# Put-off modulation sums, latent norms by halves, and a shorter last norm in a two-block transformer kernel

## Chip, cores and metric

One core of one Trainium2 chip runs the whole program in one launch. The metric is device time in microseconds (us), the median of the runs that were timed. All inputs lie in HBM and are read once; one sequence of 256 positions with 1024 features goes through.

## The reference

The first part has two layers, each with two feed-forward networks ("ffn0" to "ffn3" in the kernel) around a mixer: a windowed mean in layer 0, causal attention with 8 heads in layer 1. The second part is one block with a state-space branch, an attention branch over latents (16 heads), gates and an output projection. Every sublayer starts with an RMS norm whose scale and shift come from the conditioning vector `c`:

```python
c_silu = jax.nn.silu(c)
mods = jnp.split(c_silu @ ada_w[layer] + ada_b[layer], N_MOD, axis=-1)   # 1024 x 9216
h = modulate(rms_norm(x, norm_g[layer, 0]), sh, sc)                      # norm * (1 + sc) + sh
x = x + 0.5 * (1.0 + g)[:, None, :] * swiglu(h, w_in, w_out)
...
h = _rmsnorm(x, g_pre[l]) * (1.0 + scale[:, None]) + shift[:, None]
u_s, z_s, q_lat, kv_lat, k_rope, z_m, gl_s, gl_m = jnp.split(h @ w_in[l], split_at, axis=-1)
q = (_rmsnorm(q_lat, g_q_norm) @ w_q_up).reshape(bsz, seq, MLA_HEADS, QK_NOPE + QK_ROPE)
kv = (_rmsnorm(kv_lat, g_kv_norm) @ w_kv_up).reshape(bsz, seq, MLA_HEADS, QK_NOPE + V_HEAD)
...
out = merged @ w_out[l]
x = x + gate[:, None] * _rmsnorm(out, g_post[l])
```

## The kernel before

**Layout.** Everything is kept transposed: features on the 128 partitions (8 tiles, `KT`), the 256 positions along the row. Weights come as a stream of "units" of 128 x 1024 numbers (512 KB). SyncE loads a unit into one of 4 landing slots (`load_unit`, L349), ScalarE rounds it to its high part (`split_hi`, writes w_hi, L355), VectorE takes the rest (`split_lo`, writes w_lo, L359), and TensorE makes three products for each 128 x 128 block of it (`products`, L367 to L369): high by high, low by high, high by low. One unit is 24 such matmuls of 256 columns. The order on each engine is written out by hand; semaphores join them. Slot and ring have 4 entries, so a load waits for the VectorE split four units earlier, and `split_hi` waits until TensorE has used the unit four earlier.

**Modulation sums.** The conditioning products (`c_silu @ ada_w`) come in 46 blocks of 512 columns (`g_load`, 2 MB each). VectorE multiplies and adds 8 rows of a block (`g_part`, L1361 and L1364, into one of two accumulators, `g_acc`), and TensorE then sums over partitions with 4 matmuls against ones (`reduce_block`, L524, writes mods; each shows as 2 records). In a feed-forward network (`ffn`) this is done beside the 22 hidden tiles: the loops over hidden tiles (`SEGMENTS`) handle 4 tiles a pass, 12 units and 2 blocks, so TensorE meets one block every 6 units.

**Norms.** After a feed-forward network VectorE updates x, ScalarE squares it, TensorE sums the squares over partitions (`sum_squares`, L534), ScalarE takes the root (L1031 or L1338), VectorE the reciprocal (`root`, L1407), and then each tile is scaled (L1417) and split into x_hi (ScalarE, L1045) and x_lo (VectorE, L1424). `gate_coef` and `norm_coef` make the coefficients from mods.

**Latents.** In the second block the unit order is lat (4), kr (1), u (6), qup (4), kvup (4), u2 (2), zm (8). The lat tiles are normalised while TensorE does the u units: squares L1237, sums L893, root L1251, one reciprocal over 512 columns L1736, four scalings L1738, four copies to a_hi L1256, four a_lo L1715. The qup matmuls wait for all four a_lo, the kvup matmuls follow. Into this stretch fall also the sine of the rotary angles (ScalarE, L1241), the skip term of the state-space response (L1730), the storing of that response to HBM (L461) and eight loads that bring it back in shifted copies (`toep`, L469), all on SyncE's one queue.

**End.** The eight tiles of the output projection are copied from PSUM (L1100), squared (L1336), summed (L534), and after root and reciprocal VectorE scales each tile (L1884), adds it to x (L1888), and SyncE stores it (L514).

## Time and profile before

| | before |
|---|---|
| timed runs | median 1452.31 us (1451.8 to 1453.49, 3 runs) |
| the profiled execution | 1457.6 us, span 1455.8 us |
| mean granted TensorE clock | 0.964 of full |
| TensorE matmul busy | 1337.4 us, 92% of the span |
| VectorE / ScalarE / GpSimd busy | 77% / 43% / 11% |
| DMA | 318.06 MB, mean 218 GB/s |
| chain that ended last | PE 76%, DVE 12%, ACT 5%, issue 4% |

PE is TensorE, DVE VectorE, ACT ScalarE, POOL GpSimd and SP SyncE. The chain is the sequence of work followed back from the last instruction, so a share there is time that the end depends on, while a busy share alone is not. The span begins and ends with the program's instructions; the time of an execution has a little more around it.

### The profile page before, as it was taken

How to read it: one execution, taken by the hardware profiler on the slowest of the kernel's cores; microseconds unless marked ns; L12 is line 12 of the kernel's file. 1: busy time of each engine (PE TensorE's matmuls, PEld its weight loads, DVE VectorE, ACT ScalarE, POOL GpSimd, SP SyncE). 2: the span in 40 equal slices, each digit the busy share in tenths (PEclk: the TensorE clock that was granted, in tenths of full speed). 3: DMA queues.
4: the chain of work that ended last, by engine and by line, in shares of the span. 5: the costliest groups of instructions: out<-in, count | busy, mean ns of one | idle time of the engine just before them, and what ended most of it. 6: DMA issues, size and time to landing. Idle time of an engine off the chain costs nothing.

```text
span 1455.8 us, 28146 instructions
## 1 busy us (share of the span) xinstructions
PE 1337.4 (92%) x10988; PEld 1297.0 (89%) x10988; DVE 1118.1 (77%) x1697; ACT 625.0 (43%) x948; POOL 163.0 (11%) x209
## 2 busy tenths in 40 slices
PE   3899999799999897999998889999996898999996
PEld 2799998799999877999998779999996787999996
DVE  6898777797777787877777657899965777886573
ACT  3333334433333534333344553433364456355443
POOL 6891000000000020000001000000001002331000
PEclk9899999799999998999999899999998999999998
DMA  9788787278876455887753237886655278455551
GB/s 368 258 333 298 288 289 273 90 276 313 289 288 232 128 175 200 338 303 289 290 156 114 71 143 279 342 293 232 210 160 150 78 152 145 140 174 182 166 186 47
DMA packets 91286, 318.06 MB, mean 218 GB/s; under 512 B 21920, under 2 KB 34496, under 8 KB 85056
## 3 DMA queue, kind: packets, MB, share of 16 engines
q1 hardware_dynamic: 91200, 316.87, 63.7%
q8 instruction: 59, 0.97, 0.3%
q14 instruction: 27, 0.22, 0.0%
HBM read 311.82 MB, written 5.01 MB: 218 GB/s over the span
## 4 chain that ended last, share of the span: by engine, by line
PE 76%; DVE 12%; ACT 5%; issue 4%; DMA 1%; POOL 1%; SPq 0%; DVEq 0%; ACTq 0%; POOLq 0%
PE tiles L367 16%; PE tiles L369 15%; PE tiles L368 15%; PE acc L367 6%; PE acc L369 6%; PE acc L368 6%; ACT w_hi L355 2%; PE mods L524 2%; DVE arena L1364 2%; DVE w_lo L359 2%; PE nrm L534 1%; PE tiles L557 1%; PE tiles L559 1%; PE acc L677 1%; DMA land<-in_stream 1%
## 5 line engine op out<-in xcount | busy, mean ns | idle before, releaser
L359 DVE TENSOR_TENSOR w_lo<-land,w_hi 128x1024 fp32r<-128x1024 f32 x391 | 483.0, 1239 | 204.7 <-ACT w_hi L355 202.3
L355 ACT CAST w_hi<-land 128x1024 fp32r<-128x1024 f32 x391 | 408.5, 1046 | 525.6 <-PE tiles L369 286.1
L367 PE MATMUL tiles<-x_hi,w_hi 128*128 128x256 f32 x1464 | 419.3, 286 | 7.6 <-ACT arena L1100 3.9
L368 PE MATMUL tiles<-x_lo,w_hi 128*128 128x256 f32 x1464 | 415.0, 283 | 0.0
L369 PE MATMUL tiles<-x_hi,w_lo 128*128 128x256 f32 x1464 | 414.9, 283 | 0.0
L367 PEld LDWEIGHTS tiles<-x_hi,w_hi 128*128 128x128 f32 x1464 | 281.6, 192 | 11.5 <-ACT arena L1100 4.1
L368 PEld LDWEIGHTS tiles<-x_lo,w_hi 128*128 128x128 f32 x1464 | 281.6, 192 | 1.1 <-issue 1.0
L369 PEld LDWEIGHTS tiles<-x_hi,w_lo 128*128 128x128 f32 x1464 | 281.5, 192 | 0.0
L1364 DVE SCALAR_TENSOR_TENSOR arena<-arena,csil 128x512 f32<-128x512 f32 x280 | 212.5, 759 | 2.0
L367 PE MATMUL acc<-h_hi,w_hi 128*128 128x256 f32 x704 | 202.3, 287 | 0.3 <-DVE h_lo L1383 0.3
L367 PE MATMUL tiles<-a_hi,w_hi 128*128 128x256 f32 (+1 forms) x656 | 188.9, 288 | 13.7 <-DVE a_lo L1715 12.4
L369 PE MATMUL acc<-h_hi,w_lo 128*128 128x256 f32 x704 | 199.2, 283 | 0.0
L368 PE MATMUL acc<-h_lo,w_hi 128*128 128x256 f32 x704 | 199.1, 283 | 0.0
L368 PE MATMUL tiles<-a_lo,w_hi 128*128 128x256 f32 (+1 forms) x656 | 186.5, 284 | 0.0
L369 PE MATMUL tiles<-a_hi,w_lo 128*128 128x256 f32 (+1 forms) x656 | 186.5, 284 | 0.0
L367 PEld LDWEIGHTS tiles<-a_hi,w_hi 128*128 128x128 f32 (+1 forms) x656 | 125.7, 192 | 15.9 <-issue 12.8
L367 PEld LDWEIGHTS acc<-h_hi,w_hi 128*128 128x128 f32 x704 | 135.1, 192 | 0.4 <-issue 0.4
L368 PEld LDWEIGHTS acc<-h_lo,w_hi 128*128 128x128 f32 x704 | 135.1, 192 | 0.0
L369 PEld LDWEIGHTS acc<-h_hi,w_lo 128*128 128x128 f32 x704 | 135.0, 192 | 0.0
L368 PEld LDWEIGHTS tiles<-a_lo,w_hi 128*128 128x128 f32 (+1 forms) x656 | 125.8, 192 | 0.7 <-issue 0.7
L369 PEld LDWEIGHTS tiles<-a_hi,w_lo 128*128 128x128 f32 (+1 forms) x656 | 125.8, 192 | 0.0
L1100 ACT ACTIVATE arena<-tiles 128x256 f32<-128x256 f32 (+4 forms) x81 | 35.3, 435 | 102.7 <-PE tiles L369 94.8
(328 smaller groups left out, 1680.5 us busy)
## 6 DMA issues: line engine op xcount, KB each, us to landing
land<-in_stream SPq DMA_DIRECT2D x391, 512.0 KB, 4.3
arena<-in_gstream SPq DMA_DIRECT2D x46, 2048.0 KB, 8.8
w_dram<-arena SPq DMA_DIRECT2D x3, 512.0 KB, 6.3
arena<-w_dram SPq DMA_DIRECT2D x6, 256.0 KB, 11.0
x<-in_x_t SPq DMA_DIRECT2D x1, 1024.0 KB, 14.0
arena<-in_ssm_bn SPq DMA_DIRECT2D x1, 1024.0 KB, 5.6
u_dram<-arena SPq DMA_DIRECT2D x1, 1024.0 KB, 5.3
arena<-u_dram SPq DMA_DIRECT2D x8, 128.0 KB, 6.3
```

The source lines that it names most:

```text
L355: nc.scalar.copy(w_hi[:, u % RING], land[:, u % LAND]).then_inc(hi_done, 1)
L359: nc.vector.tensor_tensor(w_lo[:, u % RING], land[:, u % LAND], w_hi[:, u % RING].bitcast(F32), ALU.subtract).then_inc(lo_done, 1)
L367: nc.tensor.matmul(outs, lh, rh, start=first, stop=False, **kw)
L368: nc.tensor.matmul(outs, lh, rl, start=False, stop=False, **kw)
L369: last = nc.tensor.matmul(outs, ll, rh, start=False, stop=end, **kw)
L524: m = nc.tensor.matmul(mods[:, bass.ds(i * 8 + (4 * b + q), 1)], g_acc[:, b % 2, q * P:(q + 1) * P], ones[:, 0:1], start=True, stop=True)
L534: m = nc.tensor.matmul(nrm[:, 0:T], ones, t_buf[:, k], start=(k == 0), stop=(k == KT - 1))
L557: nc.tensor.matmul(outs[c], lh, hi[:, k], start=(k == 0 and not (c and one_bank)), stop=False, skip_group_check=True)
L559: nc.tensor.matmul(outs[c], ll, hi[:, k], start=False, stop=False, skip_group_check=True)
L677: m = nc.tensor.matmul(acc4[:, h, qt * T:(qt + 1) * T], qq[0:parts, 2 * g + h, qt * P:(qt + 1) * P], kk[0:parts, 2 * g + h, :], start=True ...
L1100: nc.scalar.activation(dst, src, func, **kw).then_inc(freed["a"], 1)
L1364: V.scalar_tensor_tensor(out=acc, in0=rows, scalar=cv, in1=acc, op0=ALU.mult, op1=ALU.add).then_inc(g_done if k == 7 else g_step, 1)
```

## The change

Five things change. (1) The last four blocks of modulation sums of ffn0, ffn1 and ffn2, and the last two of ffn3 (`LATER`), are no longer summed by TensorE inside the loops but after the next `sum_squares` (`reduce_later`); the first twelve of them get four accumulators of their own (`late_acc`), and the loops are cut into 3 + 1 + 1 passes so that the last two can differ. `gate_coef(1, ...)` moves behind the norm since it needs one of these blocks. (2) The latent norm is made by halves and stands ahead of a weight split on VectorE; the qup matmuls wait for the two q latents alone and the kvup matmuls for the other two. (3) On SyncE the qup units are loaded ahead of the store of the response, and its eight reloads come after the first four zm units. (4) The sine is taken ahead of ffn2. (5) The last norm: the square is taken straight from PSUM, the copy applies the gain, VectorE adds seven of the eight squares so that TensorE sums in two matmuls, the root's table is fetched early, and the final scaling and addition go over 4, 2 and 2 tiles at once with three stores.

```diff
-SEGMENTS = [[(5, "silu")], [(5, "silu")], [(5, "silu")], [(1, "silu"), (1, "c2"), (1, "c2"), (1, "c2"), (1, None)]]
+SEGMENTS = [[(3, "silu"), (1, "silu"), (1, "silu")]] * 3 + [
+    [(1, "silu"), (1, "c2"), (1, "c2"), (1, "c2"), (1, None)]]
+LATER = [[11, 12, 13, 14], [23, 24, 25, 26], [34, 35, 36, 37], [44, 45]]
...
+LAST = [(0, 4), (4, 6), (6, 8)]
...
             units("u", 6)
+            units("qup", 4)
             sp.wait_ge(k_made, 1)
             sp.dma_start(k_dram.rearrange("f c m -> c f m"), ksb).then_inc(k_stored, 16)
-            units("qup", 4)
+            units("kvup", 4)
+            units("u2", 2)
+            units("zm", 4)
             sp.wait_ge(k_stored, 16)
             sp.wait_ge(tt_clear, 1)
...
+            def reduce_later(f):
+
+                pe.wait_ge(coef_done, 2 * (f + 1))
+                for b in LATER[f]:
+                    reduce_block(b)
...
-                            if vector and m % 2 == 1:
+                            if vector and m % 2 == 1 and b + m // 2 not in LATER[f]:
                                 reduce_block(b + m // 2, i)
...
             sum_squares(1)
+            reduce_later(0)
...
                 if n == 0:
-                    pe.wait_ge(al_done, 4)
+                    pe.wait_ge(al_done, 2)
...
             for n in range(4):
                 u = UNIT["kvup"] + n
                 pe.wait_ge(lo_done, u + 1)
+                if n == 0:
+                    pe.wait_ge(al_done, 4)
...
-            sum_squares(7)
+            pe.wait_ge(rt_done, 7)
+            pe.wait_ge(sq_sum, KT - 2)
+            nc.tensor.matmul(nrm[:, 0:T], ones, t_buf[:, 0], start=True, stop=False)
+            pe.wait_ge(sq_done, KT * 8)
+            nc.tensor.matmul(nrm[:, 0:T], ones, t_buf[:, KT - 1], start=False, stop=True).then_inc(nrm_done, 1)
...
+            act.wait_ge(ang_done, 3)
+            nc.scalar.activation(rope2[64:96], ang[64:96, 0:2], ACT.Sin).then_inc(sin_done, 1)
             ffn(2, 4)
...
-                if n == 3:
-                    for k in range(4):
+                if n in (2, 3):
+                    for k in (2 * n - 4, 2 * n - 3):
                         act.wait_ge(af_done, k + 1)
                         nc.scalar.copy(a_hi[:, k], lat_n[:, k]).then_inc(ah_done, 1)
...
             for n in range(KT):
-                evacuate(TILE["out"] + n, tile_of("out", n), o_raw[:, n])
+                wait_tile(act, TILE["out"] + n)
+                nc.scalar.square(t_buf[:, n], tile_of("out", n)).then_inc(sq_done, 1)
+                evacuate(TILE["out"] + n, tile_of("out", n), o_raw[:, n], ACT.Identity, scale=coef[:, 8, n:n + 1])
                 ahead()
-                wait_freed(act, TILE["out"] + n)
-                nc.scalar.square(t_buf[:, n], o_raw[:, n]).then_inc(sq_done, 1)
...
             for n in range(6):
-                ahead()
+                if n != 2:
+                    ahead()
...
                     dve.wait_ge(lrt_done, 1)
-                    link(V.reciprocal(rh[:], rh[:]))
...
+                    for q, (name, k0) in enumerate((("g_q", 0), ("g_kv", 2))):
+                        half = rh[:, q * T:(q + 1) * T]
+                        link(V.reciprocal(half, half))
+                        for k in range(2):
+                            V.scalar_tensor_tensor(out=lat_n[:, k0 + k], in0=lat_raw[:, k0 + k], scalar=vec(name, k),
+                                                   in1=half, op0=ALU.mult, op1=ALU.mult).then_inc(af_done, 1)
+                    ahead()
+                if n in (2, 3):
+                    for k in (2 * n - 4, 2 * n - 3):
+                        a_part(k, lat_n[:, k], 8 + k + 1, al_done)
...
+            for n, (a, b) in enumerate(LAST):
+                V.tensor_tensor(o_raw[:, a:b], o_raw[:, a:b], rx.unsqueeze(1).to_broadcast([P, b - a, T]),
+                                ALU.mult).then_inc(t_done, 1)
+                dve.wait_ge(t_done, KT * N_STAGES + n + 1)
+                V.tensor_tensor(x[:, a:b], x[:, a:b], o_raw[:, a:b], ALU.add).then_inc(fin_done, 1)
...
             pool.wait_ge(tt_clear, 1)
+            pool.wait_ge(al_done, 4)
+            pool.wait_ge(k_stored, 16)
             pool.wait_ge(kr_done, 1)
```

The first place is TensorE between ffn0 and the mixer (acc is PSUM, nrm the sums of squares, mods the modulation sums). Before:

```order
L367 MATMUL acc<-h_hi,w_hi 128x256
L368 MATMUL acc<-h_lo,w_hi 128x256
L369 MATMUL acc<-h_hi,w_lo 128x256
L534 MATMUL nrm<-arena,cons 128x256 x8
L367 MATMUL acc<-w_hi,x_hi 128x256
```

The same place with the change:

```order
L390 MATMUL acc<-h_hi,w_hi 128x256
L391 MATMUL acc<-h_lo,w_hi 128x256
L392 MATMUL acc<-h_hi,w_lo 128x256
L557 MATMUL nrm<-arena,cons 128x256 x8
L547 MATMUL mods<-cons,arena 128x1 x16
L390 MATMUL acc<-w_hi,x_hi 128x256
```

Sixteen short matmuls (four blocks) have come to stand between the sums of squares and the mixer's first product.

The second place is VectorE in the latent stretch, from the splits of the last u units that stand ahead of the latent norm. Before:

```order
L359 TENSOR_TENSOR w_lo<-land,w_hi 128x1024 x2
L1730 SCALAR_TENSOR_TENSOR arena<-cons,vecs,arena 128x16 x8
L359 TENSOR_TENSOR w_lo<-land,w_hi 128x1024
L1736 RECIPROCAL rh<-rh 128x512
L1738 SCALAR_TENSOR_TENSOR arena<-arena,vecs,rh 128x256 x4
L359 TENSOR_TENSOR w_lo<-land,w_hi 128x1024 x2
L1746 TENSOR_TENSOR arena<-arena,rope_tab 32x256
L1747 TENSOR_TENSOR arena<-acc,rope_tab 32x256
L1748 TENSOR_TENSOR arena<-arena 32x256
L1715 TENSOR_TENSOR a_lo<-arena,a_hi 128x256 x4
```

With the change (L382 is the split, L1781 the reciprocal, L1783 the scaling, L1758 the a_lo):

```order
L382 TENSOR_TENSOR w_lo<-land,w_hi 128x1024 x2
L1774 SCALAR_TENSOR_TENSOR arena<-cons,vecs,arena 128x16 x8
L1781 RECIPROCAL rh<-rh 128x256
L1783 SCALAR_TENSOR_TENSOR arena<-arena,vecs,rh 128x256 x2
L1781 RECIPROCAL rh<-rh 128x256
L1783 SCALAR_TENSOR_TENSOR arena<-arena,vecs,rh 128x256 x2
L382 TENSOR_TENSOR w_lo<-land,w_hi 128x1024
L1758 TENSOR_TENSOR a_lo<-arena,a_hi 128x256 x2
L382 TENSOR_TENSOR w_lo<-land,w_hi 128x1024
L1758 TENSOR_TENSOR a_lo<-arena,a_hi 128x256 x2
L382 TENSOR_TENSOR w_lo<-land,w_hi 128x1024
L1793 TENSOR_TENSOR arena<-arena,rope_tab 32x256
```

The reciprocal stands one split earlier, the first two a_lo three rows behind it, and no a_lo stands behind the key's rotation any more.

The third place is VectorE at the end of the program (arena is the projection's output). Before, the first of eight pairs:

```order
L359 TENSOR_TENSOR w_lo<-land,w_hi 128x1024 x4
L1407 RECIPROCAL arena<-arena 128x256
L1884 SCALAR_TENSOR_TENSOR arena<-arena,coef 128x256 x2
L1888 TENSOR_TENSOR x<-x,arena 128x256
L1884 SCALAR_TENSOR_TENSOR arena<-arena,coef 128x256
L1888 TENSOR_TENSOR x<-x,arena 128x256
```

With the change, to the program's end:

```order
L382 TENSOR_TENSOR w_lo<-land,w_hi 128x1024 x4
L1929 TENSOR_TENSOR arena<-arena 128x256 x6
L1449 RECIPROCAL arena<-arena 128x256
L1933 TENSOR_TENSOR arena<-arena 128x1024
L1936 TENSOR_TENSOR x<-x,arena 128x1024
L1933 TENSOR_TENSOR arena<-arena 128x512
L1936 TENSOR_TENSOR x<-x,arena 128x512
L1933 TENSOR_TENSOR arena<-arena 128x512
L1936 TENSOR_TENSOR x<-x,arena 128x512
```

Six additions of squares stand ahead of the reciprocal, and sixteen short instructions behind it have become six wider ones.

## Rows read from the trace of the kernel before

**Rows 1.** The page, busy time of each engine.

```profile
PE 1337.4 (92%) x10988; PEld 1297.0 (89%) x10988; DVE 1118.1 (77%) x1697; ACT 625.0 (43%) x948; POOL 163.0 (11%) x209
```

**Rows 2.** Chain that ended last: start, length, what; reductions in ffn0, ffn3.

```profile
223.45 0.79 PE mods L524 x8
...
241.62 0.79 PE mods L524 x8
...
948.49 0.79 PE mods L524 x8
...
1002.99 0.79 PE mods L524 x8
```

**Rows 3.** Waits of PE, 60 to 250 us: total, times, longest.

```profile
PE nrm L534 <- ACT arena L1027: 1.4, 1, 1.4
```

**Rows 4.** ScalarE in order of time, last output tiles.

```profile
1438.77 0.38 ACT L1100 ACTIVATE arena<-tiles 128x256 f32<-128x256 f32 x1 [2.05 <-PE tiles L369]
...
1441.65 0.38 ACT L1100 ACTIVATE arena<-tiles 128x256 f32<-128x256 f32 x1 [2.04 <-PE tiles L369]
```

**Rows 5.** TensorE in order of time, first products behind three norms.

```profile
260.23 0.55 PE L367 MATMUL acc<-w_hi,x_hi 128*128 128x256 f32 x1 [6.86 <-DVE x_lo L1424]
...
491.97 0.55 PE L557 MATMUL tiles<-x_hi,w_hi 128*128 128x256 f32 x1 [3.50 <-ACT x_hi L1045]
...
1069.79 0.36 PE L557 MATMUL tiles<-x_hi,w_hi 128*128 128x256 f32 x1 [1.10 <-ACT x_hi L1045]
```

**Rows 6.** Windows: length, busy PE, PEld, DVE, ACT, POOL, granted clock, DMA.

```profile
256.00:266.00 10.00, 5.77 (x27) 5.80 (x28) 9.34 (x20) 4.51 (x10) 0.00 (x0) 0.50 0.00 0
...
1117.70:1122.90 5.20, 5.10 (x24) 5.13 (x25) 1.13 (x2) 0.59 (x1) 0.00 (x0) 0.51 0.32 101
```

**Rows 7.** VectorE in order of time, gate coefficients behind ffn0.

```profile
251.09 0.16 DVE L1389 TENSOR_TENSOR coef<-mods,vecs 128x8 f32<-128x8 f32 x1
```

**Rows 8.** VectorE in order of time, latent stretch.

```profile
1094.85 1.25 DVE L1730 SCALAR_TENSOR_TENSOR arena<-cons,vecs,arena 128x16 f32<-128x16 f32 x8
...
1103.53 3.35 DVE L1736 RECIPROCAL rh<-rh 128x512 f32<-128x512 f32 x1
...
1106.91 1.67 DVE L1738 SCALAR_TENSOR_TENSOR arena<-arena,vecs,rh 128x256 f32<-128x256 f32 x4
...
1112.87 4.83 DVE L1715 TENSOR_TENSOR a_lo<-arena,a_hi 128x256 fp32r<-128x256 f32 x4
```

**Rows 9.** ScalarE in order of time, latent stretch.

```profile
1093.69 1.28 ACT L1251 ACT_TABLE_LOAD   x1
...
1097.39 0.38 ACT L1100 ACTIVATE arena<-tiles 128x256 f32<-128x256 f32 x1 [1.71 <-PE tiles L369]
...
1101.30 1.05 ACT L355 CAST w_hi<-land 128x1024 fp32r<-128x1024 f32 x1 [3.53 <-DMA land<-in_stream]
```

**Rows 10.** TensorE in order of time, first qup product.

```profile
1117.80 0.50 PE L367 MATMUL tiles<-a_hi,w_hi 128*96 128x256 f32 x1 [11.81 <-DVE a_lo L1715]
```

**Rows 11.** SyncE: the reloads' issues in time, and its wait to store u.

```profile
1099.59 9.07 SPq L469 DMA_DIRECT2D arena<-k_dram  x8
...
SPq L474 <- ACT arena L1100: 28.0, 1, 28.0
```

**Rows 12.** ScalarE in order of time, ahead of ffn2.

```profile
563.76 1.05 ACT L355 CAST w_hi<-land 128x1024 fp32r<-128x1024 f32 x1 [4.50 <-PE tiles L564]
```

**Rows 13.** The chain that ended last, end of the program.

```profile
1441.62 3.47 PE nrm L534 x16
```

**Rows 14.** VectorE and SyncE in order of time, end of the program.

```profile
1445.61 1.75 DVE L1407 RECIPROCAL arena<-arena 128x256 f32<-128x256 f32 x1 [12.82 <-ACT arena L1338]
...
1452.92 0.42 DVE L1890 TENSOR_TENSOR x<-x,arena 128x256 f32<-128x256 f32 x1
...
1448.64 5.20 SPq L514 DMA_DIRECT2D out_t<-x  x8
```

**Rows 15.** Groups by line, a wide VectorE product: busy us, mean ns.

```profile
L1461 DVE TENSOR_TENSOR arena<-arena,ssm_s 128x1024 f32<-128x1024 f32 x5 | 6.1, 1220 | 0.0
```

More of the change, by code:

```diff
@@ L308, in build_program, with acc_of, acc_before @@
         done_sem = {"used": used, "part": part_done}
+        def acc_of(b):
+            if b in LATE_ACC:
+                return late_acc[:, LATE_ACC[b][1]]
+            return g_acc[:, b % 2]
+        def acc_before(b):
+            if b in LATE_ACC:
+                f, n = LATE_ACC[b]
+                return LATER[f - 1][n] if f else -1
+            same = [o for o in range(b % 2, b, 2) if o not in LATE_ACC]
+            return same[-1] if same else -1
         def wait_tile(eng, o):
@@ L511, in _ @@
                 load_unit(sp, u, u % LAND)
-            for k in range(KT):
-                sp.wait_ge(fin_done, k + 1)
-                sp.dma_start(out[:, k], x[:, k]).then_inc(out_st, 16)
-            sp.wait_ge(out_st, 16 * KT)
+            for n, (a, b) in enumerate(LAST):
+                sp.wait_ge(fin_done, n + 1)
+                sp.dma_start(out[:, a:b], x[:, a:b]).then_inc(out_st, 16)
+            sp.wait_ge(out_st, 16 * len(LAST))
         @block.tensor
@@ L751, in _ @@
             sum_squares(3)
+            reduce_later(1)
             first_columns(UNIT["kv"], TILE["k"], KT * 3)
@@ L774, in _ @@
             sum_squares(4)
+            reduce_later(2)
             def q_unit(h):
@@ L866, in _ @@
             sum_squares(6)
+            reduce_later(3)
             def lag_step(f):
@@ L1402, in norm_coef @@
                                             in1=vec(gname, g0, 8), op0=ALU.add, op1=ALU.mult))
-                link(V.tensor_tensor(coef[:, stage, 8:16], mods[:, sh:sh + 8], vec("bias", sh, 8), ALU.add))
+                V.tensor_tensor(coef[:, stage, 8:16], mods[:, sh:sh + 8], vec("bias", sh, 8),
+                                ALU.add).then_inc(coef_done, 1)
+                dve.wait_ge(coef_done, stage + 1)
             def root(n):
@@ L1498, in ffn @@
                     b += 2 * reps if vector else 0
-                blocks[0] = b
+                blocks[0] = b - len(LATER[f])
                 split_lo(dve, o_unit(base, 21))
@@ L1511, in ffn @@
                 norm_coef(next_stage)
+                blocks[0] = b
                 split_lo(dve, ahead_units[2])
@@ L1542, in _ @@
             norm_t(1)
+            gate_coef(1, 40, vec("pool_scale", 0, 8))
             for k in range(4, 8):
@@ L1749, in _ @@
                     dve.wait_ge(kr_done, 1)
-                    dve.wait_ge(af_done, 4)
-                    for k in range(4):
-                        a_part(k, lat_n[:, k], 8 + k + 1, al_done)
             for n in range(4):
```

39 lines of the change are left out of this document (15 added, 24 removed).

## Prediction

> **What bounds the kernel now.** I read the page first: TensorE's matmuls are busy 92% of the span, VectorE's instructions 77% [rows 1]. A busy matmul engine need not be the limit, so I took the chain that ended last. It runs through TensorE for most of its length, and inside the feed-forward networks it shows a fixed rhythm: the sums of a modulation block return every 18.17 us in ffn0 (241.62 - 223.45) and three such steps take 54.50 us in ffn3, again 18.17 each [rows 2]. The list of waits for 60 to 250 us says the same from the other side: TensorE waits 1.4 us in nearly the whole of ffn0 and the norm behind it [rows 3]. So in these loops TensorE is the bound, and what is taken from it there is gained in full. Outside the loops it stands still at the norms, where it waits for x_hi or x_lo (6.86 us behind ffn0, 3.50 us behind ffn1, the same behind ffn2, 1.10 us behind ffn3 where other small products fill the gap) [rows 5], in the latent stretch for 11.81 us [rows 10], and at the end of the program, where the last product is over at 1441.62 [rows 13] and the rest is a serial tail.
>
> **Sums put off.** What one block costs TensorE in the loop: between two blocks stand 6 units. A unit takes 2.88 us, seen undisturbed in the output projection, whose tiles are fetched at 1438.77 and 1441.65 [rows 4]. 18.17 - 6 x 2.88 = 0.89 us; the chain itself gives the block 0.79 [rows 2], and the first matmuls behind it start a little late. 14 blocks leave the loops: 14 x 0.89 = 12.5 us (11.1 by 0.79). VectorE still multiplies them, so I ask whether it now binds: a pair of tiles asks it for 6 splits of about 1.22 [rows 15] and 8 multiply-adds, and TensorE had no wait on it [rows 3]; a step shorter by 5% leaves that so.
>
> They come back behind the norms. Four blocks are 3.2 to 3.6 us. Behind ffn0 they fit into 6.86 us. Behind ffn1 and ffn2 they fit into 3.50 us or overrun by 0.1; the first eight x_hi tiles then come at ScalarE's pace, so that such a lateness is mostly made up: 0.1 us lost in all. Behind ffn3 two blocks (1.6 to 1.8 us) stand where only 1.10 us is idle: 0.5 to 0.7 us late, of which I count 0.2. What is queued behind `reduce_later` is the next stage's first product; what it waits for, `coef_done`, comes from VectorE's coefficients, made before the squares are summed. `gate_coef(1)`, two instructions of 0.16 us with a wait between them [rows 7], leaves the path from ffn0 to the mixer's norm: 0.3 gained.
>
> **The clock behind ffn0.** From 256 to 266 us the granted clock is 0.50, the level of 1.2 GHz, after TensorE stood still from 253.4; it has work again from 260.23 [rows 5], and in the 5.77 busy us it does 27 matmuls [rows 6]. At full clock 27 x 2.88 / 24 = 3.2 us, so this costs 2.5 us. With four blocks in front the idle stretch is about 3.4 us. Whether the clock then stays up is open: in the row behind ffn1 it was 3.50 us. Bounds 0 and 2.5; I take 1.2, and 0.3 for the two norms whose gaps are filled. The Trainium skill ("TensorE: Matmul & The Clock Gate", What's actually happening) has it that the throttled state is the default and activity releases it, by which the filled gaps should help; whether matmuls of one column count as activity neither it nor a row here shows. Sum of this part: 0.3 + 1.2 + 0.3 - 0.1 - 0.2 = 1.5.
>
> **Latent norm.** TensorE's last u product hands over at 1105.8 (1117.80 less the pause), and the first qup product waits for the fourth a_lo, which ends at 1117.70 [rows 8, 10]. Followed back: the a_lo stand behind two more splits and the key's rotation; these behind a reciprocal of 3.35 us at 1103.53; this behind a split at 1102.4 whose high part ScalarE began only at 1101.30, after 3.53 us of waiting for a load [rows 8, 9]. The load was late because SyncE issued it behind the store of the response, which waits for L1730, over at 1096.10. Now the load stands ahead of that store and needs only the split four units earlier, and the reciprocal doesn't wait for the split. VectorE from 1096.10: half a reciprocal 1.75 (that of 256 columns [rows 14]), two scalings 1.67 / 2, and the same again, 1101.3; the split 1.2, 1102.5; two a_lo at 0.42 each (the price of this shape at the end [rows 14]), 1103.4; at the 1.21 that they took before [rows 8] 1105.0. Its high part ScalarE can make once the third u unit is through, 1097.39 [rows 9]. The root, which came behind a table load that ended at 1094.97, is no later, and that load of 1.28 us [rows 9] falls away with the sine. So all is there 0.8 to 2.4 us before TensorE asks, and the pause of 11.8 us goes to nothing. The next split and the other two a_lo end by 1105.6 to 1107, and the kvup matmuls want them 4 x 2.88 = 11.5 us after 1105.8. The load of the first kvup unit waited for the reloads; now it waits for the split at 1102.5, still some 14 us ahead of its use.
>
> With the pause goes its clock: from 1117.7 to 1122.9 TensorE did 24 matmuls in 5.2 us at 0.51 [rows 6] instead of in 2.88: 2.3 us. Sum 11.8 + 2.3 = 14.1; bounds 0 (something else holds the qup products as long) and 14.1.
>
> **What is moved past queues.** The eight reloads take SyncE 9.07 us [rows 11]. They now stand behind the fourth zm load, where SyncE waited 28.0 us for the last u2 tile before it stored u [rows 11]. They fill 9 of these 28 us. Their data is wanted in the gates stage, long behind: nothing. The sine with its table load, about 1.9 us, stands ahead of a split for which ScalarE waits 4.50 us [rows 12]: nothing; without that cover 1.9. GpSimd's copy of the rotated key waits for more, but its readers are the attention scores: nothing.
>
> **End.** The eight sums took 3.47 us from 1441.62 [rows 13], 0.43 each. Now one is done at once, the other waits for the last square (about 0.4 from 1441.65), so the root can start near 1442.7 instead of 1445.1: 2.4 gained. The early table costs nothing, ScalarE has idle stretches there. Scaling and adding lasted from 1447.4 to 1453.3, 5.9 us [rows 14]; six wide ones are 2 x 1.22 [rows 15] and four of half that width at about 0.7 (an estimate, half and a little), with waits 5.4: 0.5 gained. Lost: a tile's bank is held by the square for 0.4 before the copy frees it, which the third output tile feels once, 0.4; the last store carries twice the bytes, 0.4 (bounds 0 and 1). Net 2.1.
>
> **Sum.** 12.5 + 1.5 + 14.1 + 0 + 2.1 = 30.2. The profiled execution took 1457.6 us (span 1455.8) and would take 1427.4. It is 5.3 us above the median of the timed runs, 1452.3, which becomes 1422.1.
>
> **Rivals.** (A) Another wait takes the latent one's place: for, VectorE has only 0.8 to 2.4 us in hand and ScalarE does the copies between its splits; against, each step of the new order is earlier by itself. If 4 to 12 us stay, the time is 1426 to 1436. Chance 0.12. (B) The put-off sums cost at the norms what they cost in the loops, as they would if the x_hi products lose their start: the 12.5 us return, 1434. Against it the gaps of 6.86 and 3.50. Chance 0.05. (C) The clock stays up behind ffn0 and at other norms: the 2.5 in place of 1.2, and about 1 us (an estimate, under half of 2.5) at each of the two others: 1419. Chance 0.10. (D) Not faster: cutting each loop into three gives every engine six more loop bodies that are run once. If each entry stalls TensorE by 5 us, 6 x 5 = 30 eats everything, and above that the kernel is slower (1426 at 0.6 us each). The rows speak against it: in ffn3, whose loops are all run once, the rhythm is 18.17 as in ffn0 [rows 2], so a stall above some hundredths isn't there. The Trainium skill ("Runtime: NRT & Kernel Launch", Instruction fetch mechanics) says that a taken branch out of the prefetched pages stalls an engine until the page has come; the rhythm doesn't show it. Chance 0.02.
>
> **How the numbers follow.** The forecast has the rest, 0.71, with 1418.5 to 1425.5 of its own from 11.1 or 12.5 for the blocks, 0 to 2.5 for the clock and 0 to 1 for the last store. To leave out no more than 2 in 10 the range takes in C and the near part of A: 1416 to 1430. A measurement of this kernel can tell about 0.2% (3 us) from no change; every case but D is beyond it: faster 0.97, within 0.01, slower 0.02.
>
> **What would show it.** In the trace of the changed kernel: blocks in the last two passes of each of ffn0 to ffn2 gone and 17.3 us for six units there; sixteen mods matmuls between nrm and the next product, over before x_hi; no idle ahead of the first qup product, and a clock of 1.0 behind it; the reciprocal at the end about 2.4 us after the last product. I am wrong if TensorE waits before qup or kvup for a split or an a_lo, if the first products behind the norms start later than before relative to the sums of squares, or if the half clock falls elsewhere and takes its price back.

## The result and the profile after

The changed kernel takes 1427.41 us, the median of 4 runs (1425.52 to 1429.94), beside 1452.6 us (1451.8 to 1453.49) for the kernel before on the same chip: a ratio of 0.9828, 95% interval 0.9810 to 0.9845. Measured again later, it gave 0.9829 (0.9816 to 0.9843). It is 25.0 us faster, 22.5 to 27.6. Forecast were 1422.1 and a range of 1416 to 1430: faster, as said, and within the range, but 5 us of the promised 30.2 are not there.

The profiled execution of the changed kernel took 1425.52 us, 1.9 below its median; that of before had stood 5.3 above its own. So the two profiled executions differ by 32.1 where the medians differ by 25.2, and no stage should be judged by these two alone. I come back to this below.

The page, to be read against [rows 1]:

```profile
PE 1327.5 (93%) x10976; PEld 1289.2 (91%) x10976; DVE 1117.0 (78%) x1694; ACT 623.1 (44%) x948; POOL 164.1 (12%) x209
```

The chain that ended last (start, length, what), beside [rows 2]: the sums of the blocks that stayed, and the put-off ones.

```profile
79.06 0.79 PE mods L547 x8
97.22 0.79 PE mods L547 x8
...
169.89 0.79 PE mods L547 x8
...
482.43 3.78 PE mods L547 x32
...
1051.95 1.68 PE mods L547 x16
```

The rhythm is as before (97.22 - 79.06 = 18.16), and after the block at 169.89 ffn0 has no more of them. What six units then take is read from ScalarE's fetches of every second hidden tile:

```profile
215.02 0.38 ACT L1094 ACTIVATE arena<-tiles 128x256 f32<-128x256 f32 x1
...
232.30 0.38 ACT L1094 ACTIVATE arena<-tiles 128x256 f32<-128x256 f32 x1
```

232.30 - 215.02 = 17.28, the 17.3 that the prediction named as its sign; ffn1 and ffn2 show 17.28 as well. The put-off ones follow the sums of squares without a gap: 16 products (2 records each) in 3.78 us behind ffn1 and in 3.46 behind ffn2, 8 in 1.68 behind ffn3.

TensorE in order of time, the first products behind the norm of ffn0, beside [rows 5] (in brackets the idle time before a row; where there is none, TensorE came straight from the row above):

```profile
247.91 3.69 PE L557 MATMUL nrm<-arena,cons 128*128 128x256 f32 x16 [2.26 <-ACT arena L1066]
251.44 3.63 PE L547 MATMUL mods<-cons,arena 128*128 128x1 f32 x32
258.13 0.55 PE L390 MATMUL acc<-w_hi,x_hi 128*128 128x256 f32 x1 [3.06 <-DVE x_lo L1466]
```

The same behind ffn1:

```profile
484.86 1.35 PE L547 MATMUL mods<-cons,arena 128*128 128x1 f32 x8
486.07 0.56 PE L586 MATMUL tiles<-x_hi,w_hi 128*128 128x256 f32 x1
```

Behind ffn0 the gap is 3.06 instead of 6.86 us, behind ffn1 there is none. New is the 2.26 ahead of the sums of squares, a wait for ScalarE.

The latent stretch, VectorE in order of time, beside [rows 8]:

```profile
1084.90 0.88 DVE L1783 SCALAR_TENSOR_TENSOR arena<-arena,vecs,rh 128x256 f32<-128x256 f32 x2
...
1086.83 0.76 DVE L1758 TENSOR_TENSOR a_lo<-arena,a_hi 128x256 fp32r<-128x256 f32 x2
...
1088.63 0.76 DVE L1758 TENSOR_TENSOR a_lo<-arena,a_hi 128x256 fp32r<-128x256 f32 x2
```

And TensorE, the first qup product, beside [rows 10]:

```profile
1090.35 0.28 PE L390 MATMUL tiles<-a_hi,w_hi 128*96 128x256 f32 x1
```

The first qup product starts at 1090.35 behind the last u product, with no idle time, where [rows 10] has 11.81. The first two a_lo end at 1087.6, 2.8 us ahead of it, and the other two a_lo, which the kvup products want, at 1089.4.

The end, ScalarE in order of time, beside [rows 13]:

```profile
1412.20 0.38 ACT L1374 ACTIVATE arena<-tiles 128x256 f32<-128x256 f32 x1 [2.13 <-PE tiles L392]
...
1413.37 0.47 ACT L1378 ACTIVATE arena<-nrm,cons 128x256 f32<-128x256 f32 x1 [0.43 <-PE nrm L1044]
```

VectorE, beside [rows 14]:

```profile
1413.94 1.75 DVE L1449 RECIPROCAL arena<-arena 128x256 f32<-128x256 f32 x1 [3.71 <-ACT arena L1378]
1415.73 1.23 DVE L1933 TENSOR_TENSOR arena<-arena 128x1024 f32<-128x1024 f32 x1
...
1420.18 0.69 DVE L1936 TENSOR_TENSOR x<-x,arena 128x512 f32<-128x512 f32 x1
```

The reciprocal starts 1.74 us after the start of the last square (1412.20), where it took 1445.61 - 1441.65 = 3.96 from the last tile's fetch to it. The second term, the wide products, is there too: 1415.73 to 1420.87 is 5.1 us for what took 5.9.

### The profile page after: what moved, and what is told of

Read it like the earlier page. It is cut to its first block, busy times and chain, and to the rows that moved or that the text cites. A ratio compares the mean times of both kernels' runs of the same rounds, so it can differ in the third digit from the quotient of the medians.

```text
span 1423.7 us, 27600 instructions
## 1 busy us (share of the span) xinstructions
PE 1327.5 (93%) x10976; PEld 1289.2 (91%) x10976; DVE 1117.0 (78%) x1694; ACT 623.1 (44%) x948; POOL 164.1 (12%) x209
## 4 chain that ended last, share of the span: by engine, by line
PE 80%; DVE 10%; ACT 5%; issue 3%; POOL 1%; DMA 1%; DVEq 0%; ACTq 0%; SPq 0%; POOLq 0%
PE tiles L390 17%; PE tiles L392 16%; PE tiles L391 16%; PE acc L390 6%; PE acc L392 6%; PE acc L391 6%; ACT w_hi L378 2%; PE mods L547 2%; DVE arena L1404 2%; DVE w_lo L382 2%; PE nrm L557 2%; PE tiles L586 1%; PE acc L706 1%; PE tiles L588 1%; DVE rh L1605 1%
## 5 line engine op out<-in xcount | busy, mean ns | idle before, releaser
L382 DVE TENSOR_TENSOR w_lo<-land,w_hi 128x1024 fp32r<-128x1024 f32 x391 | 484.6, 1243 | 181.7 <-ACT w_hi L378 179.3
L547 PEld LDWEIGHTS mods<-cons,arena 128*128 128x128 f32 x368 | 47.1, 201 | 27.8 <-issue 15.0
## 6 DMA issues: line engine op xcount, KB each, us to landing
x<-in_x_t SPq DMA_DIRECT2D x1, 1024.0 KB, 13.9
```

The source lines that it names most:

```text
L382: nc.vector.tensor_tensor(w_lo[:, u % RING], land[:, u % LAND], w_hi[:, u % RING].bitcast(F32), ALU.subtract).then_inc(lo_done, 1)
L547: m = nc.tensor.matmul(mods[:, bass.ds(i * 8 + (4 * b + q), 1)], acc_of(b)[:, q * P:(q + 1) * P], ones[:, 0:1], start=True, stop=True)
```

## The parts one by one

The diff falls into three groups that work alone. I ran each on top of the kernel before, and the kernel before beside them, unchanged, for a second profile.

> The kernel before, unchanged, against itself. Both theories: ratio 1.000 within 0.15%, about 1452.5 us. Its profile is what is wanted: in the first profiled execution (1457.6 us, 5.3 above the median) the rows added up to 104 us at half clock, 13.7 of them at 800 to 814. If the missing 5 us of the forecast are a peculiarity of that execution, this one shows fewer half-clock stretches and a time near the median; the latent pause of 11.8 us and the block price of 0.89 us stay the same.

Measured: 1452.92 (12 runs), ratio 0.9997 (0.9986 to 1.0008); its profiled execution took 1455.88. Its pause ahead of qup is 11.6 us. Its mean granted clock is 0.967, so some 96 us at half clock, against 0.964 and some 105 in the first profile (an estimate, twice what the mean lacks of 1 times the span): fewer, as expected, but this execution too stands 3.0 us above its median. The same program moves by itself: from the norm behind ffn3 to the latent root the first profile needed 1094.99 - 1066.33 = 28.7 us, this one 27.5.

> The kernel before with the latent part alone (halves of the reciprocal, order on VectorE and ScalarE, reload order, sine, GpSimd's waits). Theory 1, each term as forecast: 14.1 us less, 1438.5. Theory 2, the half clock behind the pause was no real cost because a stretch at half clock comes back elsewhere: the pause alone, 11.8 us less, 1440.8. Theory 3, most of the 25 us measured came from here and the sums gave little: 17 us or more less, under 1436.

```diff
             units("u", 6)
+            units("qup", 4)
             sp.wait_ge(k_made, 1)
             sp.dma_start(k_dram..., ksb)
-            units("qup", 4)
+            units("kvup", 4)
...
-            for k in range(4):
-                a_part(k, lat_n[:, k], 8 + k + 1, al_done)     # in unit 4
+            if n in (2, 3):
+                for k in (2 * n - 4, 2 * n - 3):
+                    a_part(k, lat_n[:, k], 8 + k + 1, al_done)
```

These are its main lines; the halves of the reciprocal, the earlier sine and GpSimd's two waits belong to it too. Measured: 1441.9 (6 runs), ratio 0.9916 (0.9899 to 0.9933), which is 12.2 us less, between 9.7 and 14.7. What TensorE waits for from 1085 to 1260 us in the kernel before, second profile (total, times, longest):

```profile
PE tiles L367 <- DVE a_lo L1715: 11.6, 1, 11.6
PE acc L677 <- DVE arena L1609: 4.4, 1, 4.4
```

And in this kernel:

```profile
PE acc L677 <- DVE arena L1611: 4.4, 1, 4.4
```

The first row is gone and the others are untouched, to the tenth. By the traces: from the root behind ffn3 to the last root, four profiles of kernels whose latent part is the old one show 378.8 and 377.4 us (before), 378.5 (loops cut, below) and 376.9 (sums part, below), 377.9 in the mean, and this one 364.0. That is 13.9 less, 11.6 of it the pause; the other 2.3 fit the clock's price of the forecast. The clock bears this out: in all five profiles that have the pause it falls to 0.50 within the pause and stays there for the first 3.5 to 6.1 us of qup products, half of which, 1.7 to 3.1 us, is lost (worked out from these lengths); here it is 1.00 from the norm behind ffn3 to 1145, and the changed kernel's two profiles have it at 1.00 there too. By the time it is 12.2, with 11.8 (theory 2) and 14.1 both inside the interval, so only the traces speak for theory 1.

> The kernel before with the put-off sums alone (loops cut 3+1+1, 14 blocks behind the norms, gate_coef(1) behind norm_t). Theory 1: 12.5 for the blocks and 1.5 for the norms and their clock, 14.0 us less, 1438.6. Theory 2, no clock gain: 12.3 less, 1440.3. Theory 3, each block costs TensorE less than 0.89 us or the loop entries take some back: 7 to 10 us less, 1442.6 to 1445.6.

```diff
-SEGMENTS = [[(5, "silu")], [(5, "silu")], [(5, "silu")], ...
+SEGMENTS = [[(3, "silu"), (1, "silu"), (1, "silu")]] * 3 + ...
+LATER = [[11, 12, 13, 14], [23, 24, 25, 26], [34, 35, 36, 37], [44, 45]]
...
             sum_squares(1)
+            reduce_later(0)
```

Measured: 1444.18 (6 runs), ratio 0.9927 (0.9908 to 0.9945), 10.6 us less, between 8.0 and 13.4. The forecast of 14.0 lies outside. Theory 2, no clock gain and 12.3, is inside; theory 3 (7 to 10) is partly inside, but its reasons, a cheaper block or loop entries, fail below.

> The kernel before with the last norm alone (squares from the tile, sums of squares on VectorE, three wide scalings and stores). Theory 1: 2.1 us less, 1450.5. Rival: the VectorE additions and the bank held by the square cost what the eight matmuls cost, 0 to 1 us less; 1451.6 to 1452.6. In the trace the reciprocal should start about 4.0 us behind the last product's tile, where it took [rows 13, 14] 1445.61 less 1441.65.

```diff
-            sum_squares(7)
+            pe.wait_ge(sq_sum, KT - 2)
+            nc.tensor.matmul(nrm[:, 0:T], ones, t_buf[:, 0], start=True, stop=False)
+            pe.wait_ge(sq_done, KT * 8)
+            nc.tensor.matmul(nrm[:, 0:T], ones, t_buf[:, KT - 1], start=False, stop=True)
```

Measured: 1450.34 (12 runs), ratio 0.9981 (0.9969 to 0.9994), 2.8 us less, between 0.9 and 4.5. ScalarE and VectorE in order of time:

```profile
1437.05 0.38 ACT L1343 ACTIVATE arena<-tiles 128x256 f32<-128x256 f32 x1 [2.13 <-PE tiles L373]
...
1438.80 1.75 DVE L1416 RECIPROCAL arena<-arena 128x256 f32<-128x256 f32 x1 [3.72 <-ACT arena L1347]
```

The square of the last tile starts at 1437.05, the reciprocal 1.75 us later: 2.2 us better than before, against 2.4 forecast. The time alone leaves the rival (0 to 1 us) room; these rows don't.

The three add up: 12.2 + 10.6 + 2.8 = 25.6, and all together measure 25.0. Each part is known to 2 or 3 us only, so a small loss between them can't be excluded; within that, what is missing is missing inside the parts.

## Whether cutting the loops costs anything

> The sums part with its lists of put-off blocks empty: loops cut into 3+1+1 and gate_coef(1) moved, every block summed in its loop as before. It isolates what cutting the loops costs (rival D of the prediction). Theory 1, the entries are free: 0 to 1 us less than before, 1452 to 1453. Rival: each of the six added loop bodies stalls TensorE; at 0.5 us each 3 us more, 1456, which would be the 3.4 us that the sums part missed (14.0 forecast, 10.6 measured). In the trace ffn0 from root to root shows the cost directly: 224.8 us before.

```diff
-LATER = [[11, 12, 13, 14], [23, 24, 25, 26], [34, 35, 36, 37], [44, 45]]
+LATER = [[], [], [], []]
```

Measured: 1452.99 (12 runs), ratio 0.9995 (0.9984 to 1.0006). All six together cost 0.9 us at most, by the interval. ffn0 from root to root is 224.4 us (224.8 before). That removes rival D, and it makes this kernel one more control for the table that follows.

Every norm has one root on ScalarE (`ACTIVATE arena<-nrm`), so the distance between two roots is the length of a stage, free of where the run began. Six profiles are of kernels without put-off sums (two of before, loops cut, the latent part, the latent order below, the last norm), three are with them (the sums part and two of the changed kernel). Means, with lowest and highest, in us:

| stage, root to root | six without | three with | difference |
|---|---|---|---|
| ffn0 | 225.3 (224.4 to 226.3) | 222.0 (221.9 to 222.1) | -3.3 |
| mixer | 23.6 (23.0 to 24.3) | 23.0 (22.6 to 23.7) | -0.6 |
| ffn1 | 210.5 (210.2 to 210.9) | 206.7 (206.5 to 207.1) | -3.8 |
| behind ffn1, to the key norm | 15.3 (14.5 to 15.8) | 16.1 (16.1 to 16.2) | +0.8 |
| ffn2 | 235.7 (235.4 to 236.2) | 232.7 (232.0 to 233.1) | -3.0 |
| behind ffn2 | 92.9 (92.4 to 93.8) | 93.7 (92.7 to 94.2) | +0.8 |
| ffn3 | 207.9 (206.1 to 210.1) | 206.0 (204.4 to 207.8) | -1.9 |

The four networks give 12.0 us, 0.86 for each of 14 blocks; forecast were 12.5 at 0.89. The three stretches behind ffn0, ffn1 and ffn2, where the sums now stand, lose 1.0 together by these means, where the forecast had a gain of 1.7 (0.3 + 1.2 + 0.3 - 0.1). Behind ffn3 only the sums part isolates them, 376.9 against 377.4 to 378.8 to the last root: no loss, in one profile. The loops are as computed, by the rhythm of 17.28 too; the norms are not.

How large their loss is, is less sure than the means say, since their half-clock stretches differ in length. Behind ffn1 the clock is at 0.50 for 3.4 us in both profiles of before and for 6.8 us in the other seven of the table. At 6.8 us the stage is 15.7 without the sums and 16.1 with them; at 3.4 us it is 14.5 without, and 14.7 and 14.6 in two later kernels with sums (the fill and the first swap of loads, below). So the sums cost 0.1 to 0.4 us there. Behind ffn2 half of the 0.8 stands between two roots of the attention, where nothing was changed and where every kernel shows either 22.5 or 23.7 us. With like set beside like the three stretches are even, to a few tenths: the promised gain is missing, but hardly more.

## The norms: clock, load and order

Windows of TensorE around the first products behind ffn1 (length; busy PE, PEld, DVE, ACT, POOL with instructions; granted clock; DMA share, GB/s), the kernel before, second profile:

```profile
488.00:492.00 4.00, 0.62 (x3) 0.19 (x1) 2.81 (x4) 1.94 (x4) 0.00 (x0) 0.94 0.42 131
492.00:496.00 4.00, 3.88 (x22) 3.91 (x23) 4.00 (x11) 2.77 (x7) 0.00 (x0) 0.64 0.00 0
```

The sums part:

```profile
484.00:488.00 4.00, 4.00 (x20) 4.00 (x21) 4.00 (x11) 2.77 (x7) 0.00 (x0) 0.50 0.02 4
```

TensorE there, in order of time, its put-off sums:

```profile
480.45 4.75 PE L543 MATMUL mods<-cons,arena 128*128 128x1 f32 x32
```

Before, TensorE idles for 3.4 us of four and then does 22 products in the next four, at 0.64. With the sums in the gap it is busy all the time, but in the four us that hold the end of the sums and the first products the clock is 0.50, the level of 1.2 GHz, and of the 20 records 6 are of one-column products and 14 of the first products of 256 columns. The gap is filled and the clock falls as it did behind an idle one. It even falls within the sums: they take 4.75 us, where they take 3.6 at full clock, and the first product behind them starts 4.4 us after the root (4.4 too in the second profile of the changed kernel, 3.6 in its first), where all six profiles without the sums have 3.5. That the first products start later than before was one of the prediction's signs of being wrong, and behind ffn1 it came. Behind ffn0 the half-clock stretch is 10.2 us in both profiles of before and 6.8 in those of the changed kernel, but it is 6.8 in the four other kernels without put-off sums as well, so this isn't theirs. Over the whole kernel I added up, in windows of 1 us, TensorE's busy time times what the clock lacks of 1.00: 32.7 and 31.2 us in the two profiles of before, 28.2 with the last norm alone, 27.7 with the loops cut, 27.4 with the latent part, 32.5 with the sums part, 25.3 and 31.5 in the two profiles of the changed kernel, 24.9 with the fill that follows. Programs that hardly differ are 5 us apart in it, and so are two executions of one. A gain of 1.2 or 2.3 us from the clock, read off one profile, is within that.

One experiment makes the gap busy in another way.

> The changed kernel with 22 idle products of 128 columns (ones by ones, into free columns of the bank of the sums, read by nobody) behind the put-off sums of ffn0 and behind the norm ahead of ffn3, where TensorE waits 3.1 and 3.5 us. It tests what the prediction left open: whether the half clock behind a norm can be held off by work in the gap. Theory 1: at 256 to 264 and 850 to 856 the granted clock is 1.00 instead of 0.5 in part, 1 to 1.7 us gained at each, about 1425. Rival (the clock's stretches come anyway and only shift): sum of the loss unchanged, time within 0.5 us of the changed kernel.

```diff
+            def fill(stage, n):
+                pe.wait_ge(rt_done, stage + 1)
+                for _ in range(n):
+                    nc.tensor.matmul(nrm[:, 384:512], ones, ones, start=True, stop=True)
...
             reduce_later(0)
+            fill(1, 22)
...
             sum_squares(5)
+            fill(5, 22)
```

Windows behind ffn0, in the second profile of the changed kernel:

```profile
254.00:256.00 2.00, 1.35 (x7) 1.26 (x6) 2.00 (x7) 1.87 (x5) 0.00 (x0) 0.50 0.00 0
...
260.00:262.00 2.00, 2.00 (x16) 2.00 (x15) 1.86 (x6) 0.00 (x0) 0.00 (x0) 0.81 0.01 4
```

With the fill:

```profile
254.00:256.00 2.00, 2.00 (x20) 2.00 (x20) 1.97 (x5) 0.71 (x2) 0.00 (x0) 1.00 0.00 0
...
260.00:262.00 2.00, 2.00 (x20) 2.00 (x19) 1.93 (x7) 0.00 (x0) 0.00 (x0) 1.00 0.00 0
```

From 256 to 260 the pair is 0.50 and 1.00. In the last window TensorE has 20 records instead of 16, but 8 of them are still the fill's. From 852 to 858 it is the same, 0.50 and 1.00. So the clock can be held, in this one profile at both places. But the time doesn't follow: 1429.38 (1427.13 to 1436.74, 5 runs), ratio 0.9842 (0.9817 to 0.9867), no better than the changed kernel. The reason is in TensorE's own order, behind the put-off sums:

```profile
255.76 5.16 PE L570 MATMUL nrm<-cons 128*128 128x128 f32 x44
260.68 0.36 PE L390 MATMUL acc<-w_hi,x_hi 128*128 128x256 f32 x1
```

The 22 products (each shows as 2 records) take 5.16 us, longer than the gap of 2.5 to 3.1 that they were to fill, and the mixer's first product has to wait for them: it starts 8.2 us after the root, where both profiles of the changed kernel have 6.5. Ahead of ffn3 the fill takes 5.18 us, and the first product starts 5.5 us after the root instead of 3.5. So the fill gave back 1.7 and 2.0 us of what it gained. The mixer takes 23.1 us from root to root, with 22.7 and 23.7 without the fill. Less the 1.7, or less what its products lose to the half clock there (1.5 and 2.7 us), all three come to 21.0 to 21.4, an estimate of what the mixer would take at full clock with a fill that ends in time. Theory 1 had the clock right; its gain was not refuted but spent by the length of the fill, and a shorter fill is untested.

Behind ffn0 there is a second cause, the wait of 2.26 us. The chain of the changed kernel there:

```profile
236.13 0.33 SPq L408
236.50 8.38 DMA land<-in_stream
244.90 1.05 ACT w_hi L378
245.97 1.28 ACT L1063
...
247.91 3.71 PE nrm L557 x16
```

VectorE multiplies its part of block 14, SyncE may then issue the load of block 16 (2 MB) and behind it, in its own order, a weight unit at 236.50; that takes 8.38 us to land; ScalarE splits it, loads its table, squares, and TensorE sums. TensorE is not in this chain. The kernel before has the same wait of ScalarE (2.90 us, at 246.89 in its second profile), and TensorE waited 1.6 us there, 1.4 in [rows 3]. Its loop is now shorter by the sums, VectorE's by nothing, and the wait grows. The four blocks of ffn0 give 3.3 us instead of 3.55, and the wait is 0.7 to 0.9 us longer.

> The changed kernel with one swap in SyncE's order behind ffn0: the two pool weight loads go ahead of the 2 MB load of block 15. In every profile so far ScalarE waited there 2.7 to 2.9 us for that weight, whose load is issued behind the block's, and TensorE's sums of squares then waited up to 2.3 us. Theory 1 (this load path, not TensorE, ends ffn0): the split begins at ScalarE's own pace, the root is 1.0 to 1.6 us earlier, 1426 against 1427.4; in the trace the wait for the load is gone. Rival: the updates of x on VectorE end at the same time and hold the sums as long: under 0.3 us.

```diff
                 if f == 0:
-                    g_load(G_POOL)
                     units("pool", 2)
+                    g_load(G_POOL)
```

Measured: 1431.52 (5 runs), ratio 0.9836 (0.9819 to 0.9853): 1.2 us behind the changed kernel by the ratios, which can't be told from nothing. ScalarE in order of time:

```profile
246.32 1.04 ACT L378 CAST w_hi<-land 128x1024 fp32r<-128x1024 f32 x1 [4.15 <-DMA land<-in_stream]
...
254.75 0.47 ACT L1070 ACTIVATE arena<-nrm,cons 128x256 f32<-128x256 f32 x1 [3.41 <-PE nrm L557]
```

SyncE, its queue:

```profile
231.14 5.28 SPq L408 DMA_DIRECT2D arena<-in_gstream  x2
236.47 12.96 SPq L372 DMA_DIRECT2D land<-in_stream  x5
```

The wait for the load is 4.15 us instead of 2.70, and the root comes at 254.75 instead of 251.64. Of these 3.1 us 1.45 are the longer wait; the rest is the clock, which falls to 0.50 while TensorE idles, so that the sums of squares take 5.38 us instead of 3.69. I had taken the wrong unit: the awaited one is the first of ffn1, whose load now stood behind two blocks of 2 MB. The error confirms the path with the other sign.

> The changed kernel with the swap that the last try missed: the first weight unit of ffn1, for which ScalarE waits 2.7 us behind ffn0, is issued ahead of the 2 MB load of block 16 and of that load's wait for VectorE, not behind both (236.50 in the profile of the changed kernel). Theory 1 (this load ends ffn0): no wait of ScalarE at 242.2, TensorE's wait of 2.3 us for the squares gone, the root 2 to 3 us earlier and the time 1424.5 to 1425.5. Rival (the updates of x on VectorE or the bandwidth, since the same bytes move, hold the norm as long): under 0.5 us.

```diff
+                if f == 1:
+                    load_unit(sp, base, base % LAND)
                 if G_FIRST[f]:
                     g_load(b)
```

ScalarE in order of time:

```profile
241.84 1.06 ACT L378 CAST w_hi<-land 128x1024 fp32r<-128x1024 f32 x1 [0.67 <-PE acc L392]
...
248.59 0.47 ACT L1072 ACTIVATE arena<-nrm,cons 128x256 f32<-128x256 f32 x1 [1.73 <-PE nrm L559]
```

VectorE:

```profile
248.51 2.33 DVE L1406 SCALAR_TENSOR_TENSOR arena<-arena,csil 128x512 f32<-128x512 f32 x3
250.75 1.75 DVE L1451 RECIPROCAL arena<-arena 128x256 f32<-128x256 f32 x1
```

TensorE:

```profile
256.73 0.55 PE L390 MATMUL acc<-w_hi,x_hi 128*128 128x256 f32 x1 [4.71 <-DVE x_lo L1468]
```

ScalarE waits no more for a load, and the root is 2.1 to 2.3 us earlier than in the two profiles of the changed kernel, counted from the first root of each (219.8 us after it, against 222.1 and 221.9). But VectorE reaches its reciprocal only at 250.75, 1.7 us behind the root's end, because three multiplications of block 15 stand ahead of it; the mixer's first product, at 256.73, is 0.5 to 0.7 us earlier by the same count. Measured: 1427.96 (5 runs), ratio 0.9822 (0.9807 to 0.9836), 1.0 us from the 0.9829 of its group, which can't be told from nothing. Theory 1 holds for the root, the rival for the time.

> The changed kernel with ScalarE's table load (1.28 us, ahead of the squares at six norms) moved behind the squares, into the 1.7 us for which ScalarE waits for the sums. Theory 1 (ScalarE is on the path at the norms that TensorE reaches with a wait for the squares: 2.3 us behind ffn0, 1.1 us behind the first attention, about 0.4 at the others): 2.5 to 4 us less than the changed kernel, 1423.4 to 1425. Rival: VectorE's updates of x end last at most of these norms: under 1 us.

```diff
-                nc.scalar.activation(eps_root, con("eps", 1), ACT.Sqrt)
                 for k in range(KT):
                     ready(k)
                     nc.scalar.square(t_buf[:, k], x[:, k])
...
+                nc.scalar.activation(eps_root, con("eps", 1), ACT.Sqrt)
```

Measured: 1424.21 (1422.83 to 1425.62, 5 runs), ratio 0.9799 (0.9786 to 0.9813), 4.3 us less than the changed kernel by the difference of the ratios, to some 3 us either way. Theory 1 said 2.5 to 4. All engines in order of time, behind ffn0:

```profile
245.75 2.55 ACT L1065 ACTIVATE arena<-x 128x256 f32<-128x256 f32 x8
...
246.30 3.69 PE L557 MATMUL nrm<-arena,cons 128*128 128x256 f32 x16 [0.78 <-ACT arena L1065]
...
248.31 1.28 ACT L1068 ACT_TABLE_LOAD   x1
```

The squares start at 245.75 at the end of the split, the wait of TensorE is 0.78 instead of 2.26, and the table load lies under the sums. From the first root to the last this kernel takes 1380.8 us, the changed one 1383.9 and 1387.2 in its two profiles; 1.8 of the smaller difference stands between the first root and the end of the first mixer, most of the rest in tenths at the other networks. How much of the larger one is the clock's I can't say. That is the fastest kernel of the study.

> The changed kernel with the table load behind the squares (alone 0.9799 of before, where the changed kernel has 0.9829) and the first weight unit of ffn1 ahead of block 16 (alone 0.9822). If the two add up: 0.9799 less 0.0007, 0.979, about 1423.5. Rival: behind ffn0 both work on the same path, which now ends in VectorE's order (last update of x, split, three parts of block 15, then the reciprocal), so that the second gives nothing there: 0.980, 1424.5.

Measured: 1425.51 (5 runs), ratio 0.9803 (0.9784 to 0.9823): by the time both the rival's 0.980 and the 0.979 of the sum are possible. The trace speaks for the rival: from the first root to the mixer's first product it takes 229.9 us, where the table edit alone takes 227.7, so the second edit brings nothing there.

## Whether the loads mattered in the latent stretch

> The latent part without its moves past queues: the halves of the reciprocal and the new order on VectorE and ScalarE are made, but the reloads of the response, the sine and GpSimd's copy stay where they were before. Theory 1 (the load is on the path, as the prediction traced it): the split that the response's reloads delay still comes late, ScalarE copies the a_hi behind it, so part of the pause stays: 4 to 9 us of the 11.8, ratio of about 0.995. Rival (the halves alone do it): pause at nothing and 12.2 us less as with the whole part, 0.9916.

The diff is that of the latent part without its lines in SyncE's program, the sine and GpSimd's two waits.

Measured: 1447.97 (6 runs), ratio 0.9963 (0.9949 to 0.9976), 5.4 us less (3.5 to 7.4), where the whole latent part has 12.2. SyncE in order of time:

```profile
1096.01 9.14 SPq L469 DMA_DIRECT2D arena<-k_dram  x8
1105.20 21.80 SPq L349 DMA_DIRECT2D land<-in_stream  x9
```

ScalarE:

```profile
1097.34 1.05 ACT L355 CAST w_hi<-land 128x1024 fp32r<-128x1024 f32 x1 [3.12 <-DMA land<-in_stream]
...
1110.47 1.04 ACT L355 CAST w_hi<-land 128x1024 fp32r<-128x1024 f32 x1 [4.54 <-DMA land<-in_stream]
1111.42 1.07 ACT L1102 ACTIVATE arena<-tiles 96x512 f32<-96x512 f32 x2
```

TensorE:

```profile
1112.15 0.50 PE L367 MATMUL tiles<-a_hi,w_hi 128*96 128x256 f32 x1 [3.83 <-ACT arena L1102]
```

The reloads keep SyncE for 9.14 us from 1096.01, the weight behind them lands so late that ScalarE waits 4.54 us for it, the fetch of a tile stands behind that split, and TensorE waits 3.83 us for the fetch. A second load wait of 3.12 us, ahead of the reloads, is that of [rows 9]. So the qup pause itself went by the order on VectorE and ScalarE, but the late load makes a new one at kvup, and from 1112 to 1116 the clock is 0.57. From the root behind ffn3 to the last root it takes 369.9 us, 5.9 more than with the whole part. Theory 1 holds in size (6.8 us stay by the time, 5.9 by the trace, 4 to 9 forecast) and the rival, that halves alone do it, falls. The place was not as I had it: I expected a remnant at qup.

## Why the prediction was right, and by how much it was off

- **The bound.** TensorE bounds the four networks: 14 blocks taken out of it give 12.0 us against 12.5. "What is taken from it there is gained in full" holds inside the loops, where six units without a block take 17.28 us, the forecast's 18.17 less 0.89. It fails at the end of ffn0, where the chain runs from VectorE through a load and ScalarE. The wait of 1.4 us in [rows 3] was its sign, and I passed over it.
- **The clock behind ffn0 and the filled gaps.** This is the step that failed: it promised 1.5 in sum, 1.7 of it behind ffn0, ffn1 and ffn2, and those three stretches show a loss of 1.0 by the means and no gain when like is set beside like. The half clock was taken for a price of idling that one-column sums could lower. The windows show 0.50 around them, and behind ffn1 it lengthens the sums themselves from 3.6 to 4.75 us, which "or overrun by 0.1" had not allowed for. The 0.3 for `gate_coef(1)` did come: from the root to the mixer's first product it takes 6.5 us in the loops-cut kernel, the sums part and the changed kernel, where that call was moved, and 6.7 to 6.9 in the kernels where it was not. With a price that varies by 6 us between executions, the clock should have entered the range and not the sum.
- **Latent.** Right to the row: a_lo two by two ahead of the products, no pause, no new wait. 14.1 forecast, 12.2 (9.7 to 14.7) by the time, 13.9 by the trace. (The last u product hands over at 1106.0, not 1105.8; nothing hangs on it.) The pause is 11.3 to 11.8 in the five profiles that have it.
- **Reloads, sine and GpSimd at nothing.** Right in the direction that was asked: moved, they cost nothing visible. That the old order of the reloads holds up a load was in the prediction as a reason; the run that keeps it (and the sine and GpSimd's copy in their places) is 6.8 us slower than the whole part, and its trace shows the load's wait at kvup.
- **End.** 2.1 forecast, 2.8 (0.9 to 4.5) measured.
- **Rivals.** A: no wait took the latent one's place. B: the sums cost 1 us at the norms at most, not 12.5. C, the clock stays up, is refuted with the sums alone, and where a fill made it true the fill itself took the time back. D: 0.9995.
- **The base.** All terms were read off an execution 5.3 us above its median, and the sum was then taken from the median as if none of them belonged to that excess. The 1.5 us of clock and norms are of the kind that differs between executions; the 2.3 of clock behind the latent pause went with the pause in every profile. The forecast's own range of 1418.5 to 1425.5 is not quite its terms either: they give 1420.4 at the low end (1.3 from the clock and 0.4 from the store). Of the 5.2 us between 30.2 and the measured 25.0, the norms account for 2.7 by the stage means, for about 2 when like is set beside like, and the loops for 0.5. The rest, 2.0 to 2.7, the intervals hold, and I can't assign it.

What stays open: how much of the 25.0 us is due to the clock, since its stretches come and go by the execution, those last 2 to 3 us, and what a fill no longer than its gap would bring.

## What to carry to other kernels

Split a large diff into parts that run alone: here they add up to 0.6 us, and the stage lengths from one landmark to the next, over several profiles, showed in which stretch a forecast failed, where any two traces would have misled. Even then compare like with like: means over few profiles mixed half-clock stretches of 3.4 and 6.8 us. When a wait is filled, ask which chain ends there next: behind ffn0 it was a load whose issue waited for another engine, and at every norm a table load that could lie under the sums. Take half-clock time as a spread, not as a term, unless a run shows that it goes with the wait. And when filler work brings nothing, first look whether it ended in time: here it ran 1.7 and 2.0 us over.

## What was not expected of the hardware

- TensorE was granted 0.50 in four us in which it was busy throughout, with the end of 16 one-column products and the first products of the stage behind ffn1 (the sums part, 484 to 488), and 1.00 where 22 products of 128 columns followed such sums (254 to 260 with the fill; 0.50 without it in one profile, and 0.50 from 258 in the other).
- TensorE's time lost to the half clock varied between 25.3 and 31.5 us in two executions of the same program.
- Holding the clock at 1.00 behind ffn0, where TensorE otherwise lost 2.2 to 2.7 us to the half clock by the windows, and ahead of ffn3 is possible with 22 products of 128 columns at each place, but they take 5.16 and 5.18 us, and the ratio was 0.9842 with them and 0.9829 without.
- The half-clock stretch behind ffn1 was 3.4 us long in some profiles and 6.8 in others, whatever the kernel, and the stage longer by 1.2 to 1.5 us with it.
